# Two placement edits in a two-layer mixer kernel: latent attention's score products at one weight tile, and the second layer's input transposes in two groups of four jobs

## What is computed

```python
def _layer(x, mem, positions, w_in, ...):
    (r_q, r_k, r_v, a_cq, a_ckv, a_kpe, l_x, l_v, l_o, l_i, l_f, c_q, z) = _split_cols(x @ w_in, IN_SPLITS)
    ret = _merge(_head_norm(_retention(...), ret_norm_g))
    mla = _merge(_mla(a_cq, a_ckv, a_kpe, ...))
    ...                                  # mLSTM cell, memory attention
    y = jnp.concatenate([ret, mla, mls, memo], axis=-1) * jax.nn.silu(z)
    y = y @ w_out
    return _layernorm(DEEPNORM_ALPHA * x + y, ln_g, ln_b)

def _causal_attention(q, k, v):          # latent attention: 4 heads, 2 blocks of 128 queries
    sc = jnp.einsum('bhqd,bhkd->bhqk', qblk, k)
    sc = jnp.where(kpos[None, :] <= qpos[:, None], sc, -jnp.inf)
    p = jax.nn.softmax(sc, axis=-1)
    return jnp.einsum('bhqk,bhkd->bhqd', p, v)
```

## Time and profile before

| what | value |
|---|---|
| time, median of three runs | 892.7 us |
| range of the runs | 892.56 to 893.01 us |
| span of the profiled execution (first to last instruction) | 891.0 us |
| PE busy | 884.9 us, 99% |
| DVE busy | 661.6 us, 74% |
| ACT busy | 490.7 us, 55% |
| granted TensorE clock | 1.00 in all 40 slices |

### The profile page before, as it was taken

The page is one execution under the profiler, slowest core; times in us unless marked ns, Lnnn a source line. Parts: engine busy times, 40 slices in busy tenths (PEclk is TensorE's granted clock), DMA queues, the critical chain, the costliest instruction groups (busy, mean ns, idle before and its releaser), DMA issues.

```text
span 891.0 us, 13209 instructions
## 1 busy us (share of the span) xinstructions
PE 884.9 (99%) x4548; PEld 759.8 (85%) x4548; DVE 661.6 (74%) x1312; ACT 490.7 (55%) x914; POOL 18.0 (2%) x18
## 2 busy tenths in 40 slices
PE   9999999999999999999999999999999999999997
PEld 8888998888888888888888889888888888888896
DVE  6869697877685677766668887968778747689865
ACT  6655775545555346544476556746354653575551
POOL 0000000000000000000000000000000001000001
PEclk9999999999999999999999999999999999999999
DMA  9796498447778687665665966875485865976932
GB/s 358 276 340 201 144 268 271 153 139 226 234 232 287 212 244 254 209 190 191 191 192 187 310 227 171 282 248 158 145 268 177 287 197 154 286 228 230 339 98 94
DMA packets 69650, 198.19 MB, mean 222 GB/s; under 512 B 8136, under 2 KB 21712, under 8 KB 68944
## 3 DMA queue, kind: packets, MB, share of 16 engines
q1 hardware_dynamic: 69008, 196.31, 67.8%
q10 hardware_dynamic: 576, 1.05, 0.4%
HBM read 182.38 MB, written 14.95 MB: 221 GB/s over the span
## 4 chain that ended last, share of the span: by engine, by line
PE 98%; issue 1%; DMA 0%; ACT 0%; POOL 0%; DVE 0%; POOLq 0%; ACTq 0%; DVEq 0%
PE acc L1335 24%; PE acc L1336 24%; PE acc L1339 24%; PE acc L1350 10%; PE acc L1356 5%; PE work L1102 1%; PE work L1101 1%; PE work L1100 1%; PE work L1240 1%; PE work L1239 1%; PE work L1095 1%; DMA B<-in_mem_t 0%; PE work L1262 0%; PE work L1251 0%; PE work L1179 0%
## 5 line engine op out<-in xcount | busy, mean ns | idle before, releaser
L1059 ACT ACTIVATE hi<-raw 128x512 fp32r<-128x512 f32 (+2 forms) x607 | 358.1, 605 | 317.1 <-PE acc L1339 255.5
L1422 DVE TENSOR_TENSOR lo<-raw,hi 128x512 fp32r<-128x512 f32 (+2 forms) x607 | 388.7, 657 | 174.5 <-ACT hi L1059 165.4
L1335 PE MATMUL acc<-hi,xx 128*128 128x512 f32 (+2 forms) x768 | 285.9, 375 | 0.0
L1336 PE MATMUL acc<-hi,xx 128*128 128x512 f32 (+2 forms) x768 | 283.6, 372 | 0.0
L1339 PE MATMUL acc<-lo,xx 128*128 128x512 f32 (+2 forms) x768 | 223.0, 372 | 0.0
L1335 PEld LDWEIGHTS acc<-hi,xx 128*128 128x128 f32 x768 | 144.6, 188 | 23.6
L1336 PEld LDWEIGHTS acc<-hi,xx 128*128 128x128 f32 x768 | 144.7, 188 | 23.5
L1339 PEld LDWEIGHTS acc<-lo,xx 128*128 128x128 f32 x768 | 140.4, 188 | 24.6
L1350 PE MATMUL acc<-xx,hi 128*128 128x512 f32 x384 | 96.1, 392 | 0.0
L1350 PEld LDWEIGHTS acc<-xx,hi 128*128 128x128 f32 x384 | 69.3, 189 | 12.6
L1356 PEld LDWEIGHTS acc<-xx,lo 128*128 128x128 f32 x384 | 52.4, 190 | 3.7
(11 more groups left out here) (348 smaller groups left out, 972.7 us busy)
## 6 DMA issues: line engine op xcount, KB each, us to landing
raw<-in_w SPq DMA_DIRECT2D x263, 512.0 KB, 4.3
B<-turn SPq DMA_DIRECT2D x80, 128.0 KB, 4.5
raw<-in_w SPq DMA_DIRECT2D x26, 256.0 KB, 2.7
turn<-B SPq DMA_DIRECT2D x12, 512.0 KB, 5.8
raw<-in_w SPq DMA_DIRECT2D x16, 328.0 KB, 3.3
turn<-Y SPq DMA_DIRECT2D x8, 512.0 KB, 5.6
Y<-in_wuq SPq DMA_DIRECT2D x2, 1152.0 KB, 8.6
Y<-in_x_t SPq DMA_DIRECT2D x4, 512.0 KB, 8.7
```

The costliest lines, as they stand in the source:

```text
L1059: act.activation(place(l, t, hi), raw[:, s, (t % 2) * w:(t % 2 + 1) * w], ACT.Copy)\
L1335: pe.matmul(o, ah[:, q], hi[:, s, 0:w], start=k == 0, stop=False, skip_group_check=name == "memv")
L1336: pe.matmul(o, al[:, q], hi[:, s, 0:w], start=False, stop=False, skip_group_check=name == "memv")
L1422: dve.tensor_tensor(place(l, t, lo), raw[:, s, (t % 2) * w:(t % 2 + 1) * w], place(l, t, hi).bitcast(F32), ALU.subtract).then_inc(lo_done. ...
```

## The change

The four score jobs of latent attention stand at tile 156 in both layers; before, heads 0 and 1 stood there and heads 2 and 3 at tile 168. The eight transpose jobs of the second layer stand at tiles 18 (jobs 0 to 3) and 28 (jobs 4 to 7); before, two each at 18, 22, 26 and 30. With them move ACT's `x_hi` steps (before 23, 24, 27, 28, 31, 32, 35, 36) and two of DVE's `x_lo` steps (job 4 from step 32 to 34, job 5 from 34 to 36). No instruction is added or removed, and the order of the jobs and so their banks stay.

```diff
 for _j in range(8):
-    _put(LATER_PE, 18 + _j // 2 * 4, "xT", _j)
+    _put(LATER_PE, 18 + _j // 4 * 10, "xT", _j)
 for _h in range(HEADS):
     _put(PE_AT, (71, 75, 81, 87)[_h], "mem_scores", _h)
-    _put(PE_AT, 156 + _h // 2 * 12, "mla_scores", _h)
+    _put(PE_AT, 156, "mla_scores", _h)
...
-    _put(LATER_ACT, 23 + _j // 2 * 4 + _j % 2, "x_hi", _j)
+    _put(LATER_ACT, (23, 24, 26, 27, 33, 34, 35, 36)[_j], "x_hi", _j)
...
-    _put(LATER_DVE, (24, 26, 28, 30, 32, 34, 37, 38)[_j], "x_lo", _j)
+    _put(LATER_DVE, (24, 26, 28, 30, 34, 36, 37, 38)[_j], "x_lo", _j)
```

## The result

The changed kernel takes 894.23 us, the median of 19 runs (893.91 to 895.88), beside 892.85 us for the kernel before in as many runs. The ratio is 1.0015, with a 95% interval of 1.0009 to 1.0022: 1.4 us slower, 0.15%.

A forecast was written before the change was run, and what follows sets the result against it. PE's own stream was taken to bound the kernel. Saved visits -0.12, eighth block +1.25 and scores +0.15 summed to +1.28 us, taking 892.7 to 894.0 us; range 892.5 to 894.8 us.

The forecast's parts named there:

- What bounds the kernel: Whole span: PE, busy 884.9 of 891.0 us; a wait in the middle is not given back later.
- the later raw tiles: Second layer, raw pairs behind tiles 37 to 39: issued about 1.5 us later by SP, costed at nothing.
- The gain of the saved visits: Transposes and scores on PE: two visits of each kind saved at 0.03 us each, -0.12 us.
- The moved PE jobs: Transposes at tiles 18 and 28, scores at 156: their data and banks are ready in time, cost nothing.
- The eighth block: Tile 38, second layer: DVE hands over the last `x_lo` late and PE waits; +1.25 us, bounds 0 and 1.6.
- The 0.05 us that I added for weights that can't be loaded ahead: Tile 38: after such a wait weights cannot be loaded behind running matmuls, so up to 0.1 us was added.
- The scores: Near tile 175, second layer: DVE's chain, shifted 2.61 us, gives `lo` late; +0.15 us, bounds 0 and 0.6.
- That DVE keeps up: Tile 38: eighth block in time, only the visits' gain left, 892.6 us; chance 0.12.
- The larger debt of the scores: Tiles 169 to 180, both layers: with 0.5 us more in each layer +2.3 us, 895.0; chance 0.12.
- The clock: The two longer transpose groups: clock falls to 1.2 GHz, +3.5 us on top of the forecast, 897.5; chance 0.02.

The follow-up runs named there:

- the kernel with the turn behind: The whole change, but second layer's turn of `memk` at DVE step 38 behind the last `x_lo`, not 36: 892.70 us beside 892.70 for the kernel before.
- the lone scores' edit: Kernel before with only the scores joined at tile 156 in both layers, transposes as before: 892.72 us beside 892.70, ratio 0.9999.
- the one with the kept `x_lo` steps: The whole change for PE, but `x_lo` at the steps of the kernel before: 892.83 us beside 892.70, ratio 1.0000.
- the transposes alone: Kernel before with only the transposes in two groups and the changed `x_hi` and `x_lo` steps; scores in two visits: 894.14 us beside 892.70, ratio 1.0016.
- the steps alone: Kernel before with only DVE's `x_lo` steps of jobs 4 and 5 moved to 34 and 36: 893.90 us beside 892.91, ratio 1.0013.
- the two with the turn twice: The whole change, and the kernel before, each with DVE's second-layer turn of `memk` done twice: 895.60 and 893.45 us beside 892.91.

## Why the prediction was right

The forecast was 894.0 us, +1.28 us on the 892.7 of three runs. Measured are 894.23 us, +1.38 on the 892.85 of nineteen; in the traces it is +1.37.

**What bounds the kernel** held: PE's stream, and the one new wait was not given back. The +1.47 us of the wait was still there at the last tile, less the 0.01 of the scores' visit. PE has no wait for a DMA either, so the later raw tiles cost nothing, as costed.

**The gain of the saved visits**, forecast 0.12 us: 0.07 for the transposes and 0.03 for the scores, 0.10 in all, which is also what the kernel with the turn behind shows. The working by starts and spacings can resolve hundredths that no time of the whole kernel can.

**The moved PE jobs** wait for nothing, as said.

**The eighth block**, forecast +1.25 us, bounds 0 and 1.6: 1.47 us. Mechanism, place and neighbour were right, and the replay of DVE's order was good to a few hundredths up to the turn. In the changed trace everything before is 1.71 us later, so `lo` 34 was forecast for 488.14 and stands at 488.16, and the turn for 493.44 and stands at 493.48. The term that was too small is what stands behind the turn: I gave its hand-over 0.04 us; it is 0.21. DVE waits there for its own signal and then counts up the semaphore that frees the accumulator. At the place itself the trace of the kernel before could not show it, because DVE waited for `hi` 37 there anyway. But the same turn of `memk` in the first layer, which starts at 51.78, shows it, and reading that row would have given the term:

```profile
53.24 1.29 DVE L1422 TENSOR_TENSOR lo<-raw,hi 128x512 fp32r<-128x512 f32 x2 [0.21 <-DVE B L1639]
```

The rest is hundredths along DVE's chain: the eighth block is signalled at 499.66, 0.24 us behind the forecast, of which the turn and its hand-over are 0.18. The 0.05 us that I added for weights that can't be loaded ahead was right in kind, as the 0.10 us behind the first matmul show, but not to be added: the weight load was due 0.12 us before its pair, at 498.20, and from there to the signal are 1.46 us, which is already the whole loss.

One reason in that paragraph was wrong, although its number was right. I let DVE idle before `lo` 34 because job 4 "is not there yet". It was there from 485.84 on, 2.3 us before `lo` 34 started. The new order of the steps alone made DVE idle, and most of the loss (1.22 of 1.47 us) comes with that order while the transposes stay where they were.

**The scores**, forecast +0.15 us: 0. This term failed, in two steps. I let PE be late by as much as its weight load was late; the lone scores' edit shows a load that is 0.17 us late and a matmul on time. And a part of the chain that I carried over, 0.26 us of idle on DVE before `lo` 165 that the profile puts down to "issue", was there in the kernel before and in the lone edit (0.28) and not in the changed kernel. It does not go with the scores' edit: the four further kernels with the scores' visits as before have none, and of the six with the scores joined it is in the lone edit and in the one with the kept `x_lo` steps (0.26, and there again a weight load that waits 0.16 us). What brings it stays open. In the changed kernel the `lo` of tile 175 was ready accordingly earlier, at 698.60 plus 0.73 against a weight load at 699.54. DVE's `lo` 165 in the kernel before, then `lo` 165 and 175 and the weight load in the changed one:

```profile
677.33 0.69 DVE L1422 TENSOR_TENSOR lo<-raw,hi 128x512 fp32r<-128x512 f32 x1 [0.26 <-issue]
```

```profile
682.71 0.69 DVE L1422 TENSOR_TENSOR lo<-raw,hi 128x512 fp32r<-128x512 f32 x1
...
698.60 1.25 DVE L1422 TENSOR_TENSOR lo<-raw,hi 128x512 fp32r<-128x512 f32 x2
```

```profile
699.54 0.41 PEld L1339 LDWEIGHTS acc<-lo,xx 128*128 128x128 f32 x2
```

The two misses, +0.22 and -0.15, nearly cancel, so the sum (+1.28, beside +1.37 in the traces) looks better than its terms. That part is luck.

**The rivals.** That DVE keeps up did not come about, but two variants show how near it was: the turn behind the last block, or the old `x_lo` steps, and the loss is gone. The larger debt of the scores was seen only with 1.3 us more DVE work in each layer; smaller amounts were not tried. The clock stayed at 1.00 with sixteen transposes in a row, in the stretch that holds both groups:

```profile
467.00:491.00 24.00, 24.00 (x124) 1.00 0.55 183
```

So what the Trainium skill states of transpose-mode work and the clock gate ("TensorE: Matmul & The Clock Gate", Part 4) took no effect on a group of 1.76 us between matmuls. No run here shows a longer one.

**A better version.** Both repaired variants keep 0.06 to 0.10 us of what the longer groups save in the trace, and neither can be told from the kernel before by time (892.70 and 892.83 beside 892.70). The edit's whole prize is below what can be measured.

## What to carry to other kernels

Where one engine is busy to 99%, joining its small jobs saves only entry and exit, here 0.01 to 0.04 us a visit. Read that from the starts of instructions before anything is moved, and set it against the hand-overs that come later. A step that is moved to later on a helping engine is not free because its data are ready and the engine has idle time on average: count that engine's work in order from where it last waits to the hand-over. When a pause of the busy engine is taken away, every helper that caught up in it has its margin cut by the length of the pause, also where the time doesn't show it yet.

## What the runs showed of the hardware

**The first microseconds differ from run to run by more than the change.** The starts of PE's first matmuls on real data, in the kernel before:

```profile
6.08 0.63 PE L1316 MATMUL acc<-hi,mm 128*128 128x256 f32 x2
6.50 0.44 PE L1323 MATMUL acc<-lo,mm 128*128 128x256 f32 x2
6.78 0.40 PE L1311 MATMUL acc<-hi,mm 128*128 128x256 f32 x2
7.02 0.40 PE L1316 MATMUL acc<-hi,mm 128*128 128x256 f32 x2
```

And in the changed kernel, whose program is the same here:

```profile
8.14 0.63 PE L1323 MATMUL acc<-lo,mm 128*128 128x256 f32 x2
8.57 0.63 PE L1335 MATMUL acc<-hi,mm 128*128 128x512 f32 x1
...
10.82 0.39 PE L1336 MATMUL acc<-hi,mm 128*128 128x512 f32 x1
11.04 0.39 PE L1335 MATMUL acc<-hi,mm 128*128 128x512 f32 x1
```

Two matmuls of 128x256, or one of 128x512, take 0.42 to 0.43 us from start to start at first and 0.22 to 0.24 us later. The step comes near 6.5 us in one execution and near 10 us in the other; before it PE had done the warm-up products (L1084) and waited 0.3 and 0.6 us for the first data. Over the twelve profiled executions the first token tiles stand at up to 1.7 us later and 0.2 us earlier than in the kernel before. The granted clock of the profile is 1.00 (2.4 GHz) there too, so that column doesn't show it; that the clock was at its lower level at first would fit the spacing, and no row here proves it. A span of one execution should be compared from behind this stretch.

**Waiting for one's own signal, and counting up a semaphore behind it.** Behind the turn of `memk` the program has both on DVE:

```python
                        dve.wait_ge(squared[name].sem, squared[name].at(l, 0))
                        dve.sem_inc(acc_sem(l, name), 2)
```

DVE stood 0.21 us there in all six kernels in which no `hi` was awaited at that place (the change, the transposes alone, the turn behind, the steps alone, and the two with the turn twice). The wait alone costs little: behind the first of the doubled turns, where only it stands, DVE goes on 0.04 us after the end (491.91 + 1.25 to 493.20), and behind an `x_lo`, which also has the wait alone, after 0.03 to 0.04 us. Nor is it the transpose: an addition of 128x512 (L1861) that is followed by both has the 0.21 us too, here in the kernel before.

```profile
504.17 0.69 DVE L1422 TENSOR_TENSOR lo<-raw,hi 128x512 fp32r<-128x512 f32 x1 [0.21 <-DVE B L1861]
```

So the 0.21 us goes with the semaphore that DVE counts up by an instruction of its own behind the wait; no kernel here leaves that instruction out. The turn of `rk`, which has neither, lets the next instruction start 1.16 us after its own start, before it has ended: 697.44 to 698.60 in the changed kernel.
